# Reordering the hand-over between two layers of a diffusion trunk: when tile 0 of the second layer's input is transposed, modulated and copied out

## The reference

```python
def modulate_project(x, mod, w_in):
    shift, scale, gate = jnp.split(mod, 3, axis=-1)
    u = (layer_norm(x) * (1.0 + scale) + shift).astype(x.dtype)
    return split_columns(u @ w_in), gate

def merge_residual(x, ys, zs, g_merge, gate, w_branch, w_out, ln_g, ln_b, alpha):
    gates = jnp.split(jax.nn.sigmoid(g_merge), N_BRANCH, axis=-1)
    merged = sum(gb * ((yb * jax.nn.silu(zb)) @ w_branch[i])
                 for i, (yb, zb, gb) in enumerate(zip(ys, zs, gates)))
    h = alpha * x + gate * (merged @ w_out)
    return (layer_norm(h) * ln_g + ln_b).astype(x.dtype)
```

## Time and profile before

| | |
|---|---|
| median of three runs | 1641.47 us (1641.40, 1641.47, 1644.78) |
| the profiled execution | 1644.78 us, its span 1643.0 us |
| mean granted clock of TensorE | 0.982 of full speed |
| PE busy | 1540.3 us, 94% of the span |
| DVE, POOL, ACT busy | 739.9 us, 629.0 us, 471.1 us |

### The profile page before, as it was taken

One profiled execution on the slowest core, in us unless ns is written; L12 is line 12 of the kernel. 1 busy time (PEld: TensorE's weight loads), 2 busy tenths in 40 slices (PEclk: granted clock), 3 DMA queues, 4 the chain that ended last, 5 costly groups with the idle time before them and its releaser, 6 DMA issues.

```text
span 1643.0 us, 22438 instructions
## 1 busy us (share of the span) xinstructions
PE 1540.3 (94%) x9011; PEld 1255.8 (76%) x9011; DVE 739.9 (45%) x1442; ACT 471.1 (29%) x1095; POOL 629.0 (38%) x504
## 2 busy tenths in 40 slices
PE   2798999999899999999999998999989999999997
PEld 2688768896588887688788876888757888877876
DVE  3266841346712361522587676116581236252256
ACT  1123740136610032320123376102572002232010
POOL 2164015540135534236772410456102554423571
PEclk9799999999999999999999999999999999999999
DMA  9121002225512222114431100223301222211421
GB/s 335 55 81 39 14 14 75 77 67 173 166 39 77 77 65 64 46 47 170 120 117 51 55 27 1 65 77 90 107 27 39 77 78 64 65 46 39 167 77 64
DMA packets 75991, 128.71 MB, mean 78 GB/s; under 512 B 16172, under 2 KB 20720, under 8 KB 75888
## 3 DMA queue, kind: packets, MB, share of 16 engines
q1 hardware_dynamic: 72416, 118.88, 23.6%
q10 hardware_dynamic: 3472, 8.39, 1.4%
HBM read 120.96 MB, written 6.30 MB: 77 GB/s over the span
## 4 chain that ended last, share of the span: by engine, by line
PE 81%; DVE 8%; ACT 4%; issue 3%; POOL 2%; ACTq 1%; DMA 1%; POOLq 0%; DVEq 0%
PE pb L962 56%; PE pb L1090 6%; PE pb L1219 4%; PE pb L987 3%; PE pb L1133 2%; PE pb L1170 2%; PE pb L918 1%; PE pb L1141 1%; PE pb L1263 1%; ACTq L1466 1%; POOL rms L806 1%; PE pb L1400 1%; POOL wsp L820 1%; ACT prc L1639 1%; DMA raw<-in_w_mod 1%
## 5 line engine op out<-in xcount | busy, mean ns | idle before, releaser
L962 PE MATMUL pb<-wsp,act_T 128*128 128x512 f32 x3060 | 719.9, 394 | 12.6 <-DVE act_T L1952 11.8
L962 PEld LDWEIGHTS pb<-wsp,act_T 128*128 128x128 f32 x3060 | 576.3, 190 | 138.7 <-issue 18.7
L817 POOL CAST wsp<-raw 128x1024 fp32r<-128x1024 f32 x128 | 136.5, 1066 | 868.6 <-PE pb L962 697.6
L820 POOL TENSOR_TENSOR wsp<-raw,wsp 128x512 fp32r<-128x512 f32 x268 | 359.0, 1360 | 10.2
L962 PE MATMUL pb<-wsp,yT 128*128 128x512 f32 x720 | 165.2, 389 | 0.0
L962 PEld LDWEIGHTS pb<-wsp,yT 128*128 128x128 f32 x720 | 135.2, 188 | 28.0
L2470 DVE SCALAR_TENSOR_TENSOR mt<-tg,pb 128x512 f32<-128x512 f32 x40 | 27.4, 686 | 230.6 <-PE pb L962 229.7
L1810 ACT ACTIVATE tg<-pb 128x512 f32<-128x512 f32 x60 | 35.9, 599 | 289.6 <-PE pb L962 289.6
L1660 ACT ACTIVATE pr<-pb,nm 128x640 f32<-128x640 f32 (+2 forms) x128 | 91.3, 713 | 4.8 <-DVE nm L2154 4.8
L1170 PE MATMUL pb<-ident,pr 128*128 128x128 f32 x480 | 74.0, 275 | 7.5 <-ACT pT L1695 6.2
L1090 PE MATMUL pb<-act_T,wsp 128*128 128x320 f32 x384 | 65.0, 323 | 7.1 <-POOL wsp L820 7.0
(11 more groups left out here) (278 smaller groups left out, 1979.3 us busy)
## 6 DMA issues: line engine op xcount, KB each, us to landing
raw<-in_w_in SPq DMA_DIRECT2D x112, 512.0 KB, 3.6
raw<-in_w_mod SPq DMA_DIRECT2D x32, 512.0 KB, 4.8
raw<-in_w_branch SPq DMA_DIRECT2D x24, 512.0 KB, 3.6
raw<-in_w_out SPq DMA_DIRECT2D x16, 512.0 KB, 3.7
stage<-in_w_mod ACTq DMA_DIRECT2D x8, 512.0 KB, 16.5
stage<-in_w_mod SPq DMA_DIRECT2D x8, 512.0 KB, 11.9
raw<-in_w_in SPq DMA_DIRECT2D x16, 256.0 KB, 5.1
xh<-in_x_sample SPq DMA_DIRECT2D x7, 512.0 KB, 7.5
```

Source lines behind the costliest of these rows:

```text
L817: pool.tensor_copy(hi, raw[:, p % 3, :, 0:width]).then_inc(raw_hi, 1)
L820: ins = pool.tensor_tensor(lo[:, j, :], raw[:, p % 3, j, 0:width], hi[:, j, :].bitcast(F32), ALU.subtract)
L962: mm = pe.matmul(dst, lhs(a, k, t), w[:, wa, j, 0:width], start=(k == 0 and n == 0), stop=(i == count - 1 and j == 1 and n == 2))
```

## The change

Instructions are neither added nor removed, except for two waits; the orders on four engines change, on all of them only around the hand-over from layer 0 to layer 1.

- PE: the eight transposes of tile 0 come after piece 2 of the last projection call, no longer after piece 0.
- ACT: `hi_piece(q + 1)` comes before `modulated(0)`; `of_kv(4)` comes before the two z pieces. `of_kv(0)` no longer waits until DVE has read `("out", 1, LT)`.
- POOL: each split of kv pieces comes one place earlier than the inverse square roots around it, `of_out(0, 3)` before the split of q[3], `of_kv(1)` after z[0] instead of after z[1].
- DVE: the statistics of tiles 0 to 2 are drawn ahead; `modulated(0)` and `remainder(0)` come after `gated` and `added` of half 0 of tiles 3 and 4; `modulated(1)` comes after `next_mean(3)`; in the rest `q_squares` and `q_path` come before the `modulated` of the tile beside them.

```diff
 # POOL
             split(kv[0])
             split(kv[1])
             of_out(0, 0)
+            split(kv[2])
             of_next(1, 0)
             of_out(0, 1)
-            split(kv[2])
+            split(kv[3])
             of_next(1, 1)
-            split(kv[3])
             of_out(0, 2)
             split(q[0])
             of_next(1, 2)
             split(q[1])
             split(q[2])
+            of_out(0, 3)
             split(q[3])
-            of_out(0, 3)
+            of_next(1, 3)
             of_out(0, 4)
-            of_next(1, 3)
             of_next(1, 4)
             for t in range(4):
                 of_q(1, t)
             split(z[0])
-            split(z[1])
             of_kv(1)
-            split(z[2])
-            split(z[3])
+            for i in range(1, 4):
+                split(z[i])
             of_q(1, 4)
 # PE
                 def first_turned(i, t):
-                    if (l, i, t) == (0, 0, T - 1):
+                    if (l, i, t) == (0, 2, T - 1):
                         here[0] = l + 1
                         turn_next(0)
 # ACT, of_kv
-                    if here[0] and t == 0:
-
-                        wait_done(act, ("out", 1, LT), 0)
 # ACT, hand-over
                     normalised(0)
                     hi_piece(q)
+                    hi_piece(q + 1)
                     modulated(0)
                     normalised(1)
-                    for i in range(1, 4):
-                        hi_piece(q + i)
+                    hi_piece(q + 2)
+                    hi_piece(q + 3)
                     of_kv(0)
...
                     of_q("A", 3)
+                    of_kv(4)
                     hi_piece(pieces.first[1, ("A", "z")])
                     hi_piece(pieces.first[1, ("A", "z")] + 1)
-                    of_kv(4)
 # DVE
                 gated(1, 0)
+                gated(1, 1)
                 added(1, 0)
                 mean(0)
-                gated(1, 1)
                 gated(1, 2)
+                added(1, 1)
+                mean(1)
                 scaled(0)
                 if l == 0:
                     next_mean(0)
-                added(1, 1)
+                added(1, 2)
+                mean(2)
+                scaled(1)
                 if l == 0:
                     next_shift(0)
-                mean(1)
-                added(1, 2)
-                scaled(1)
-                if l == 0:
                     next_mean(1)
-                    modulated(0)
-                    mean(2)
-                    remainder(0)
+                    scaled(2)
                     next_shift(1)
-                    scaled(2)
                     next_mean(2)
                     gated(0, 3)
                     gated(0, 4)
                     added(0, 3)
                     added(0, 4)
                     next_shift(2)
+                    modulated(0)
+                    remainder(0)
                     gated(1, 3)
                     gated(1, 4)
                     added(1, 3)
+                    mean(3)
+                    added(1, 4)
+                    mean(4)
+                    scaled(3)
+                    next_mean(3)
                     modulated(1)
-                    mean(3)
                     remainder(1)
-                    added(1, 4)
-                    scaled(3)
-                    mean(4)
-                    next_mean(3)
+                    scaled(4)
                     next_shift(3)
-                    modulated(2)
-                    scaled(4)
-                    remainder(2)
                     next_mean(4)
                     q_gains(1)
                     next_shift(4)
                     here[0] = 1
                     q_squares(0)
+                    modulated(2)
+                    remainder(2)
                     q_path("A", 0)
+                    q_squares(1)
+                    q_path("A", 1)
                     modulated(3)
-                    q_squares(1)
                     remainder(3)
                     q_lo("A", 0)
-                    q_path("A", 1)
-                    modulated(4)
                     q_squares(2)
-                    remainder(4)
                     q_lo("A", 1)
                     q_path("A", 2)
+                    modulated(4)
+                    remainder(4)
                     q_lo("A", 2)
                     q_squares(3)
                     q_path("A", 3)
                 else:
-                    mean(2)
                     scaled(2)
```

## The result

The changed kernel takes 1652.70 us (median of five runs, 1649.65 to 1657.70), the kernel before 1641.92 us (five runs, 1641.40 to 1644.78). The ratio is 1.0065, with a 95% interval of 1.0044 to 1.0087: slower by 10.8 us. The profiled execution took 1652.62 us, its span is 1650.8 us.

The account below looks back on a forecast made before the run. PE, busy 94% of the span, was taken to bound the kernel, so its idle time is paid in full. Delay 13.4 less 1.4 for the z pieces gave +12.0, hence 1653.5 us, range 1645 to 1661.

Parts of the forecast that it names:

- DVE's order up to* `remainder(0)`: DVE work ahead of layer 1's first tile: `remainder(0)` ends at 861.9, PE idle 11.5 us (bounds 3.0 and 13.1).
- The casts: POOL's casts of kv[2] and kv[3] left out of the sum; by the skill's rule, some 2 us more.
- the rival's +14: Rival: two POOL casts also hold DVE instructions, about 1 us each; +14, 1655.5 us, chance 0.10.
- To* `remainder(1)`: DVE from `remainder(0)`: 13.8 us plus 2.0 of meetings, 15.8; `("kv", 1)` at 877.7, delayed 13.4.
- The clock: PE after its 11.5 us wait: 2.7 us lost to slow clock, covered by 3.8 us wait before `("kv", 1)`; cost nothing.
- The forecast of the profile: PE's next timeline: about 11 us idle before layer 1's first L962, 2 to 4 us before `("kv", 1)`.
- The removed wait: ACT's `of_kv(0)`: old wait made `remainder(1)` late, 0.68 us on PE; in the new order it would have cost nothing.
- the 1.4 us at the first tile: PE's transposes two pieces later: by themselves free, late by 1.4 us at most.
- The z pieces: Gate product: waits 0.69 + 2.21 become 2.4; middle 1.4 us won (bounds -0.5 and 4.7).
- The sum: Whole kernel: 13.4 - 1.4 = 12.0 us slower, 1653.5 us against the median of 1641.47.
- From* `remainder(1)` *on: DVE under 10 us against 12 for PE's tile; PE leads again and the 13.4 us stay.
- Layer 1's* `else` *branch: End of layer 1: tiles 3 and 4, unchanged in order, set the end; cost nothing.

Follow-up runs that it names:

- the kernel without subtractions: The changed kernel, but POOL writes zeros as low parts of kv[2], kv[3] and q[0] to q[3] of layer 1; 1645.57 us, ratio to before 1.0030.
- DVE alone: The kernel before with the change's new order on DVE only; 1658.62 us against 1642.56, ratio 1.0101.
- POOL and ACT alone: The kernel before with the change's orders of POOL and ACT, `of_kv(0)` still waiting for DVE; 1649.98 us against 1642.56, ratio 1.0047.
- the change without DVE's part: The changed kernel with DVE in the order of before and `of_kv(0)` waiting for DVE again; 1655.84 us against 1642.71 before, ratio 1.0080.
- the kernel with `remainder(0)` earlier: The changed kernel with `modulated(0)` and `remainder(0)` before `gated(0, 3)` on DVE, `of_kv(0)` waiting for DVE again; 1654.56 us, ratio to before 1.0072.
- the weaker wait: The kernel before with `of_kv(0)` on ACT waiting for DVE's read of (out, 0, LT) instead of (out, 1, LT); one run, 1638.72 us beside 1645.49.
- PE's transposes alone: The kernel before with only PE's eight transposes moved from after piece 0 to after piece 2; 1647.83 us against 1642.56, ratio 1.0030.
- the halves: DVE's new order alone in the kernel before, ratio 1.0101; and the changed kernel with DVE's old order and `of_kv(0)` waiting for DVE, 1.0080.
- two moves out of the same change: The kernel before with `q_squares(2)` before `modulated(4)` and `remainder(4)` behind `q_path(2)` on DVE; 1639.15 us against 1642.71, ratio 0.9973.

## Why the prediction was right, point by point

- *DVE's order up to* `remainder(0)`: forecast 36.9 us from 824.99 (28.4 of list, 1.3 behind the square roots, 7.2 of meetings), measured 36.9 from 825.13: 7.9 of meetings, 1.16 behind the square roots, and 27.9 for the rest. The wait was forecast at 11.5 and is 11.36. With the subtractions there are six meetings of 1.0 to 1.1 us and two of 0.35 and 0.61, as forecast; the rest of the 7.9 is the cast. That the meetings are real and not a reading of the rows is shown by the kernel without subtractions (-6.9 us of wait). The mechanism was right, but that the sum agrees to the tenth is luck: 0.6 us for the cast were missing from it, and the list and the square roots were 0.6 too long.
- *The casts* (the rule of the Trainium skill's page "SBUF — State Buffer", section "Who interferes with whom", and a rival). The row at 840.35 and its like in the kernel without subtractions (1.91 each, 0.64 too long) show that a cast of POOL does hold a DVE instruction with two SBUF operands, which my sum left out. The page says so, and the trace agrees. It is one meeting of 0.64 and not two of 1, since the other cast came behind DVE's instruction and was the one that took longer (1.48 for 1.03): the rival's +14 doesn't hold.
- *To* `remainder(1)`: forecast 15.8 us, measured 878.09 - 862.21 = 15.9, with the two full meetings that were forecast (`added` 1.70 us at 863.18, `mean` 2.41 at 868.91). Delay at `("kv", 1)`: forecast 13.4, measured 13.8, of which 0.14 is there at the start of the call.
- *The clock:* forecast 2.7 us lost, covered by the second wait. The 12 matmuls from 862.21 take 5.34 us where they take 2.97, so 2.4 are lost, and the second wait is 1.38 us in place of the 3.8 forecast for a full clock: the cover held. The forecast of the profile, 2 to 4 us before `("kv", 1)`, didn't fit this sum, which leaves 1.1. In three experiments (DVE alone, POOL and ACT alone, the change without DVE's part) the dips weren't covered: they cost 3.4, 4.3 and 4.0 us in the traces, and the medians lay 2.1, 1.4 and 2.1 us above what was expected.
- *The removed wait:* right that it is worth nothing in the new order (in the kernel with `remainder(0)` earlier, which has the wait again, `of_kv(0)` is released by PE, not by DVE), wrong in the reason given for the old one. The prediction had `remainder(1)` late because of it; in truth DVE reached its own `modulated(1)` only at 860.2, and the weaker wait changed nothing.
- *PE's transposes alone:* the 1.4 us at the first tile were measured (1.44), but the cost of the step taken alone is 4.6 us, since POOL's square roots and with them the q pieces shift too. In the changed kernel PE's wait for DVE is 11 us, and none for q[1] to q[3] is left.
- *The z pieces:* z[1] 2.4 forecast, 2.59 measured; no dip followed, so that the gate product took 37.1 us and not 39.7: 2.6 won, 1.4 forecast, inside its bounds.
- *The sum:* +12.0 forecast, +11.6 in the hand-over of the two traces, +10.8 on the medians. The z term won 1.2 us more than forecast, and 0.8 of that was lost on the way there. That the medians agree as well is in part luck, with such a scatter between runs.
- *From* `remainder(1)` *on* PE leads again but for 0.33 us before `("kv", 4)`. The shift, forecast to stay unchanged up to the gate product, grew from 13.80 to 14.35 us (925.66 - 911.31).
- *Layer 1's* `else` *branch:* forecast nothing, and its end takes 30.8 us before and 30.7 after.

## What to carry to other kernels

When work is reordered ahead of the instruction that another engine waits for, add up everything that the feeding engine must do up to that point, by start-to-start times, and do the same for the next hand-over: moving the awaited instruction alone only moves the wait (7.00 and 5.47 us in place of 11.36 and 1.38). In the sum, DVE instructions with two SBUF operands that run beside POOL's subtractions count with up to 1.1 us more, the smallest ones too (1.24 for 0.14). Count the clock as well: each of PE's waits of over 4 us in these hand-overs was followed by matmuls that took 1.4 to 2.7 us too long, which is paid unless a later wait covers it. And the parts of a schedule are tuned to each other: here the halves cost 14.8 and 14.7 us alone and 11.6 together (in the traces), while two moves out of the same change gained 3.6.

## What the runs showed of the hardware

- A granted clock near the lower level followed an idle time of 2.21 us in the trace of before and of 5.05, 5.47 and 7.26 us in others. After the 2.59 us in the changed kernel it did not: the 36 matmuls behind it took 5.55 us as at full speed. After the same 2.59 us at the same place in the kernel without subtractions they took 7.09. So the length of the wait alone doesn't decide.
- Writing zeros on POOL didn't hold DVE (1.28 us beside them); the subtractions of the same size, reading two operands from SBUF, did (up to 2.41), and one cast held it for 0.64 us.
- Runs of one kernel on one core scatter more than the first three showed: 24 runs of the kernel before lay between 1638.92 and 1648.09 us. The mean granted clock goes with it: 0.988 in the fastest of them and 0.978 in the slowest. Why it differs from run to run was not looked for.
